# The samples' delta-state update of a gated-DeltaNet step: TensorE outer products replaced by rows spread over the partitions through DRAM, with the products on ScalarE and the sums on VectorE

## What is computed

```
S'    = exp(g) * S
u     = beta * (v - S'^T k)
o     = S'^T q + (q.k) u
S_new = S' + k u^T            # delta_sample, an output of the step
```

## Time and profile before

| what | value |
|---|---|
| median of three runs | 2118.62 us |
| lowest and highest | 2118.04 and 2120.09 us |
| span of the profiled execution | 2117.8 us |
| PE busy in the span | 2014.8 us, 95% |
| DVE, ACT, POOL busy | 1323.2, 941.4, 76.7 us |
| end of `su_done` to the end of the last addition of the samples' states | 201.35 to 331.5 us |
| first matmul of the feed-forward network | 388.2 us |

### The profile page before, as it was taken

The page is one execution under the profiler, slowest core; times in us unless marked ns, Lnnn a source line. Parts: engine busy times, 40 slices in busy tenths (PEclk is TensorE's granted clock), DMA queues, the critical chain, the costliest instruction groups (busy, mean ns, idle before and its releaser), DMA issues.

```text
span 2117.8 us, 27204 instructions
## 1 busy us (share of the span) xinstructions
PE 2014.8 (95%) x10121; PEld 1571.7 (74%) x10121; DVE 1323.2 (62%) x1367; ACT 941.4 (44%) x824; POOL 76.7 (4%) x94
## 2 busy tenths in 40 slices
PE   6998989899999998999799999999999999999997
PEld 4888965899996532325688888888888888888885
DVE  5854863555433211011488797887978889797884
ACT  3541000444320110000277676766767677676772
POOL 1231111000000000000000000000000000000000
PEclk8997987999999999899699999999999999999998
DMA  6231005355548678563199898998989989898990
GB/s 265 99 101 66 1 1 206 142 179 180 182 157 260 211 246 301 188 230 119 60 358 361 321 342 327 351 363 311 342 324 348 357 317 350 320 344 333 339 353 23
DMA packets 96731, 512.34 MB, mean 242 GB/s; under 512 B 10769, under 2 KB 10898, under 8 KB 44418
## 3 DMA queue, kind: packets, MB, share of 16 engines
q1 hardware_dynamic: 81936, 478.50, 60.9%
q10 hardware_dynamic: 13970, 25.46, 3.7%
q0 software_dynamic: 736, 7.21, 1.0%
HBM read 503.91 MB, written 7.21 MB: 241 GB/s over the span
## 4 chain that ended last, share of the span: by engine, by line
issue 67%; PE 27%; DVE 4%; ACT 1%; DMA 0%; SPq 0%; POOLq 0%; POOL 0%; ACTq 0%; DVEq 0%
PE bank L485 5%; PE bank L486 5%; PE bank L487 5%; PE bank L784 3%; PE bank L718 1%; PE bank L696 1%; PE bank L597 1%; PE bank L641 1%; PE bank L621 1%; PE bank L634 1%; DVE w_lo L1381 1%; PE bank L479 1%; ACT w_hi L1040 1%; DVE scr L1437 0%; PE bank L506 0%
## 5 line engine op out<-in xcount | busy, mean ns | idle before, releaser
L1750 DVE TENSOR_TENSOR w_lo<-raw_w,w_hi 128x2048 fp32r<-128x2048 f32 x336 | 768.8, 2290 | 140.8 <-ACT w_hi L1206 137.6
L1206 ACT ACTIVATE w_hi<-raw_w 128x2048 fp32r<-128x2048 f32 x336 | 644.9, 1920 | 429.0 <-PE bank L948 280.1
L946 PE MATMUL bank<-w_hi,xe_hi 128*128 128x512 f32 x896 | 365.6, 408 | 1.5 <-DVE xe_lo L1808 1.5
L948 PE MATMUL bank<-w_hi,xe_lo 128*128 128x512 f32 x896 | 350.8, 392 | 0.0
L947 PE MATMUL bank<-w_lo,xe_hi 128*128 128x512 f32 x896 | 350.2, 391 | 0.0
L486 PE MATMUL bank<-fh_lo,w_hi 128*128 128x264 f32 x704 | 201.8, 287 | 0.0
L946 PEld LDWEIGHTS bank<-w_hi,xe_hi 128*128 128x128 f32 x896 | 169.0, 189 | 36.0 <-issue 1.8
L948 PEld LDWEIGHTS bank<-w_hi,xe_lo 128*128 128x128 f32 x896 | 168.8, 188 | 36.1
L947 PEld LDWEIGHTS bank<-w_lo,xe_hi 128*128 128x128 f32 x896 | 169.2, 189 | 33.7
L946 PE MATMUL bank<-w_hi,aT_hi 128*128 128x512 f32 x448 | 177.1, 395 | 0.0
L947 PE MATMUL bank<-w_lo,aT_hi 128*128 128x512 f32 x448 | 174.6, 390 | 0.0
(11 more groups left out here) (329 smaller groups left out, 2500.9 us busy)
## 6 DMA issues: line engine op xcount, KB each, us to landing
raw_w<-in_moe SPq DMA_DIRECT2D x336, 1024.0 KB, 4.8
raw_w<-in_ffn_w SPq DMA_DIRECT2D x42, 1024.0 KB, 4.8
ring<-in_k_pages SPq DMA_DIRECT2D x96, 256.0 KB, 3.1
raw_w<-in_gdn_in SPq DMA_DIRECT2D x16, 1024.0 KB, 6.9
ring<-in_v_pages SPq DMA_DIRECT2D x64, 256.0 KB, 4.7
ring<-in_v_pages ACTq DMA_DIRECT2D x64, 256.0 KB, 4.1
ring<-in_att_in SPq DMA_DIRECT2D x4, 2048.0 KB, 7.9
ring<-in_k_pages ACTq DMA_DIRECT2D x32, 256.0 KB, 3.7
```

What stands on the lines that cost most here:

```text
L946: mm(out, hi, move_hi, start=first, stop=False)
L948: return mm(out, lo, move_hi, start=False, stop=last)
L1206: A(w_hi[:, p % SPLIT, :], raw_w[:, p % RAW, :], ACT.Copy).then_inc(split_hi, 1)
L1750: V.tensor_tensor(w_lo[:, p % SPLIT, :], raw_w[:, p % RAW, :], w_hi[:, p % SPLIT, :].bitcast(F32), ALU.subtract).then_inc(split_lo, 1)
```

## The change

The products k u^T leave TensorE. TensorE turns u alone into rows, after level 0 of the inverse (into bank 4, which level 1 may use only once VectorE has copied it out). SP writes the 64 rows of 128 values to a buffer in DRAM (32 KB), waits for that, and reads them back in four transfers of 16 rows each, each spread over all 128 partitions (8 KB per partition, 1 MB per transfer), into two buffers in turn; the third and fourth wait for the additions that read the first and second. ScalarE multiplies the 64 states by their decays (in GpSimd's place) and then the 64 spread rows by their keys, one number per partition, in place. VectorE adds four states at a time, four such additions behind each of the levels 2, 3, 5 and 6. The scaling of `ktok` moves from the head of level 3 to the head of level 1. GpSimd keeps only the two stores.

```diff
+ADD_LEVELS = (2, 3, 5, 6)
...
+        u_dram = nc.dram_tensor("u_dram", [NS * H, DK], F32, kind="Internal").ap()
...
-        wide = decT[0:64]
-        kv_rows = carve(core, 14336, 2, P)[0:64]
-
+        u_rows = decT[0:64, 0, 0:DK]
+
+        u_bc = [carve(hT[:, :, :].rearrange("p k t -> p (k t)"), 0, 16, DK),
+                carve(scr, (QKV + 2 * H) * T, 16, DK)]
...
# SP, behind the loads of gdn_out
+            sp.wait_ge(st_sb, 1)
+            sp.dma_start(u_dram, u_rows).then_inc(u_spread, 16)
+            sp.wait_ge(u_spread, 16)
+            for q in range(4):
+                if q >= 2:
+                    sp.wait_ge(snew, 4 * (q - 1))
+                sp.dma_start(u_bc[q % 2], u_dram[16 * q:16 * q + 16, :].unsqueeze(0).to_broadcast([P, 16, DK]))\
+                    .then_inc(u_spread, 16)
...
# PE, in the levels
+                    if l == 1 and g == 0:
+                        pe.wait_ge(st_sb, 1)
...
+                if l == 0:
+                    pe.wait_ge(sou, 1)
+                    nc.tensor.transpose(bank[4][0:64, 0:P], u_s, ident).then_inc(st_ps, 1)
...
# PE, behind the recurrence
-            pe.wait_ge(sou, 1)
             pe.wait_ge(w_sb, 2)
-            nc.tensor.transpose(bank[0][0:64, 0:P], u_s, ident)
-            nc.tensor.transpose(bank[0][0:64, P:2 * P],
-                                sk, ident).then_inc(st_ps, 1)
-            for i in range(16):
-                pe.wait_ge(st_sb, 2 + i)
-                if i < 2:
-                    pe.wait_ge(u_sb, 4)
-                else:
-                    pe.wait_ge(snew, i - 1)
-                mm(bank[2 + i % 2], kv_rows[:, 1, :], wide[:, i % 2, :], start=True, stop=True).then_inc(sout_ps, 1)
...
# ACT, in front of the copies of the recurrence's outputs
+            act.wait_ge(sread_ps, 1)
+            act.wait_ge(su_done, 1)
+            for i in range(NS * H):
+                ins = A(states[:, i, :], states[:, i, :], ACT.Copy, scale=row_b[:, 1, i:i + 1])
+                if i % 4 == 3:
+                    ins.then_inc(scaled, 1)
+            act.wait_ge(sou, 1)
+            for i in range(NS * H):
+                if i % 32 == 0:
+                    act.wait_ge(u_spread, 16 * (3 + i // 16))
+                u = u_bc[i // 16 % 2][:, i % 16, :]
+                ins = A(u, u, ACT.Copy, scale=sk[:, i:i + 1])
+                if i % 4 == 3:
+                    ins.then_inc(scaled, 1)
...
# POOL
-            pool.wait_ge(sread_ps, 1)
-            pool.wait_ge(su_done, 1)
-            for i in range(8):
-                s = states[:, 8 * i:8 * i + 8, :]
-                G.tensor_tensor(s, s, row_b[:, 1, 8 * i:8 * i + 8].unsqueeze(2).to_broadcast([P, 8, DK]),
-                                ALU.mult).then_inc(sdecayed, 1)
-            pool.wait_ge(st_sb, 1)
-            for i in range(16):
-
-                if i >= 2:
-                    pool.wait_ge(sout_ps, i - 1)
-                G.tensor_tensor(wide[:, i % 2, :].rearrange("p (a v) -> p a v", a=4),
...
# DVE, in the levels
-                if l == 3:
+                if l == 1:
...
+                if l == 0:
+                    dve.wait_ge(st_ps, 1)
+                    V.tensor_copy(u_rows, bank[4][0:64, 0:P]).then_inc(st_sb, 1)
+                if l in ADD_LEVELS:
+                    for n in range(4 * ADD_LEVELS.index(l), 4 * ADD_LEVELS.index(l) + 4):
+                        dve.wait_ge(scaled, 16 + n + 1)
+                        s = states[:, 4 * n:4 * n + 4, :].rearrange("p i n -> p (i n)")
+                        u = u_bc[n // 4 % 2][:, 4 * (n % 4):4 * (n % 4) + 4, :].rearrange("p i n -> p (i n)")
+                        V.tensor_tensor(s, s, u, ALU.add).then_inc(snew, 1)
...
# DVE, behind the recurrence
-            dve.wait_ge(st_ps, 1)
-            V.tensor_copy(kv_rows.rearrange("p r n -> p (r n)"), bank[0][0:64, 0:2 * P]).then_inc(st_sb, 1)
...
-            for i in range(16):
-                dve.wait_ge(sout_ps, i + 1)
-                dve.wait_ge(sdecayed, i // 2 + 1)
-                s = states[:, 4 * i:4 * i + 4, :].rearrange("p i n -> p (i n)")
-                V.tensor_tensor(s, s, bank[2 + i % 2][:, :], ALU.add).then_inc(snew, 1)
```

More of the change, by code:

```diff
@@ L336, in program @@
         core_done = sem("core_done")
-        sdiag, srow_ps, sread_ps, sdecayed, su_done, st_ps, st_sb, sou, sout_ps, snew = (
-            sem("sdiag"), sem("srow_ps"), sem("sread_ps"), sem("sdecayed"), sem("su_done"), sem("st_ps"), sem("st_sb"),
-            sem("sou"), sem("sout_ps"), sem("snew"))
+        sdiag, srow_ps, sread_ps, scaled, su_done, st_ps, st_sb, sou, u_spread, snew = (
+            sem("sdiag"), sem("srow_ps"), sem("sread_ps"), sem("scaled"), sem("su_done"), sem("st_ps"), sem("st_sb"),
+            sem("sou"), sem("u_spread"), sem("snew"))
         osq_done, osum, oroot, o_normed = sem("osq_done"), sem("osum"), sem("oroot"), sem("o_normed")
@@ L1307, in _ @@
             pool.dma_start(convs_out[:, :, CONV_W - 2, :], conv_new[:, :, :]).then_inc(stored, 16)
-            pool.wait_ge(sread_ps, 1)
-            pool.wait_ge(su_done, 1)
-            for i in range(8):
-                s = states[:, 8 * i:8 * i + 8, :]
-                G.tensor_tensor(s, s, row_b[:, 1, 8 * i:8 * i + 8].unsqueeze(2).to_broadcast([P, 8, DK]),
-                                ALU.mult).then_inc(sdecayed, 1)
-            pool.wait_ge(st_sb, 1)
-            for i in range(16):
-                if i >= 2:
-                    pool.wait_ge(sout_ps, i - 1)
-                G.tensor_tensor(wide[:, i % 2, :].rearrange("p (a v) -> p a v", a=4),
-                                kv_rows[:, 0, :].unsqueeze(1).to_broadcast([64, 4, DK]),
-                                ident[0:64, 4 * i:4 * i + 4].unsqueeze(2).to_broadcast([64, 4, DK]),
-                                ALU.mult).then_inc(st_sb, 1)
             pool.wait_ge(snew, 16)
```

## The result

The changed kernel takes 2083.21 us (median of four runs, 2081.00 to 2084.04) against 2119.13 us before (now the median of four runs, 2118.04 to 2120.09): ratio 0.9822, 95% interval 0.9808 to 0.9836, 35.9 us less. The forecast was 2079.0 us, with a range of 2074 to 2088. The profiled execution is the fastest of the four, 2081.0 us with a span of 2079.2 (2117.8 before).

What follows compares the result with a forecast made beforehand. It took VectorE, slowed by GpSimd, to bound the front and the samples' outer products on TensorE the tail. -8.3 - 1.2 + 2.5 - 32.6 = -39.6 us from 2117.8 gives 2078.2, plus 0.8 is 2079.0 us; range 2074.3 to 2088.

Steps and rivals of the forecast that it cites:

- Front: Level 0 of the inverse: without GpSimd's decay VectorE is free sooner, level 1 starts at 208.8 instead of 217.1, 8.3 us gained.
- Keys: Key scaling moved from level 3 to level 1: 1.2 us gained in level 3, nothing lost in level 1.
- the engine is then still on 1.2 GHz: Level 1: TensorE's four Y take 5.98 us instead of 3.74, so it finds the first mask ready.
- low end of the range: Whole kernel: additions free (-2.5) and level 1's Y at 2.4 GHz (-2.2), 2074.3 us.
- Additions: VectorE's 16 additions behind four levels: 0.47 us lost at each of three blocks, 1.1 behind level 6, 2.5 in all.
- Rival 1: Inverse: VectorE becomes the bound, additions all exposed, 11.0 us instead of 2.5, 2087.5 us; chance 0.07.
- Inputs and the way through DRAM: ScalarE's decays and scaled rows, and the spread transfers of u, are ready before the additions need them: no wait.
- rival 3: Spread reads from DRAM are slow, VectorE waits behind levels 2 and 5; slower than before beyond 23.6 us per transfer; chance 0.07.
- Tail: First square to the scale: 36.7 us before, 4.1 after without the outer products, 32.6 us gained.
- Behind the tail: Scale, inversion, spreading and projection: unchanged, with the same 4.3 us gap of TensorE between them.
- Rival 2: Row sums in the tail run at 1.2 GHz and take twice 3.6 us, 2082.6 us; chance 0.08.
- The step from span to median: Whole kernel: the median lies 0.8 us above the profiled span, turning 2078.2 into 2079.0 us.

Runs made afterwards that it cites:

- the pieces: Changed kernel with additions placed singly behind the groups of levels 2 to 5 and key scalings in fours behind level 1's: 2075.84 us.
- the third yardstick: The changed kernel unaltered, run beside the third group of experiments (keys or additions alone split up, further filling): 2081.37 us.
- the second yardstick: The changed kernel unaltered, run beside the second group of experiments (single pieces, filled gap, both together): 2083.39 us.
- the kernel with the front alone: Kernel before with only the 64 state decays moved from GpSimd to ScalarE, outer products left on TensorE: 2110.04 us, ratio 0.9953.
- the last experiment: Changed kernel with single pieces and filled gap, plus one 128-column matmul behind each of the root's eight spreads: 2077.62 us, ratio 0.9799.

## Why the prediction was right, and where it was off

*Front, forecast -8.3.* Right in mechanism, measured -9.25, and -9.1 alone. Counted from `su_done`, the second Z subtraction ended 0.25 us earlier than reckoned; the rest is the clock, which was back at 1.00 before level 1: the last Z products took 0.63 us and not 1.1, and the turn of u 0.1 and not 0.3.

*Keys, forecast -1.2 in level 3 and nothing lost in level 1.* The step "the engine is then still on 1.2 GHz" failed. The Y took 3.74 us, not 5.98, so the 2.2 us that the better clock gave were eaten by a wait of 1.9 for the scaling. Level 1 came out even (12.91 against 12.96) and the forecast's sum held by two errors that cancel, which is luck; the pieces show what was missed. The low end of the range had counted the Y at 2.4 GHz as 2.2 us gained, which the wait shows to be wrong too. In some executions the wait also costs 1.6 us of clock, which the forecast did not have at all. It does not explain on its own why the profiled execution lies 2.2 us under the median of its runs: the third yardstick's profile has no such fall either and is the slowest of its five (2083.38 us), and the second yardstick's has the fall and shares the lowest time of its five (2082.11).

*Additions, forecast +2.5.* Mis-sized by little: 0.48 at levels 3 and 4 as reckoned (0.47), 1.07 behind level 6 as reckoned (1.1), and 0.92 in level 6 instead of 0.47; in all 2.95. In level 6 TensorE waits 0.21 us for a mask, as in levels 3 and 4, and 0.43 us more for a subtraction. (The prediction reads the masks' start in level 3 as 4.05 us after TensorE's first Y; its rows give 244.74 - 240.80 = 3.94, and with that 0.56 per block and not 0.47.) Rival 1 (VectorE as the bound, all 11 us exposed) fell: VectorE could take the whole of the work free of charge, in pieces.

*Inputs and the way through DRAM, forecast free.* Right. The decays and the 32 scalings that follow step at 0.294 us (18.82 / 64), with 0.386 us shown for one; the row of 0.401 was right as a duration and too high as a pace. The Trainium skill, "VectorE: DVE Perf Modes", section "The TRN2 errata — SBUF-src ops pay a fixed extra latency per instruction", gives 350 cycles for 128 elements; the prediction's estimate from it, 0.29 us, is the step that this trace shows. Going against its advice on small tiles cost nothing here, since ScalarE had no other work. The spread reads land in 4.6 and 6.4 us per megabyte, within the forecast's bounds and near the 4.8 us of the feed-forward weights' loads of the same size, so rival 3 fell.

*Tail, forecast -32.6.* Measured -32.36 in the profile.

*Behind the tail, forecast 0, measured +1.46.* The step "the stages behind are unchanged" failed. The eight spreads took 7.41 us and not 6.89, the first 48 records of the projection 13.89 and not 12.95, at the same code and the same 4.33 us gap. In the 2 us in which the spreads start, the granted clock is 0.82 before (340 to 342 us) and 0.53 after (299 to 301). Rival 2 looked for the low clock in the row sums and was wrong there (3.72 us, clock 1.00); the low clock came one stage later. But the loss is not shown to belong to the change: the kernel with the front alone, products and all, has it too (53.47 us), and the changed kernel's three profiles lie between 52.52 and 53.46. What of the 1.46 us the change causes is open.

*The step from span to median, forecast +0.8.* This term was mis-sized. It compares the span of one execution with the median of others; within one execution the time lies 1.7 to 1.9 us above the span in every run on record (2081.0 against 2079.2 for the changed kernel). With 1.8 the forecast would have been 2080.0 us.

In sum the touched stretches give 38.5 us in the profiled pair against 39.6 forecast, and the medians 35.9. The last two numbers differ because the changed kernel's profiled execution lies 2.2 us under its median and the span before, with 1.8 added, 0.5 above its own. What makes executions of the changed kernel differ by such amounts was not found; level 1's clock is one part of it.

## What to carry to other kernels

Work that nobody later needs can still hold the end if it stands in front of needed work in an engine's order; look for the first instruction behind it and ask what that one really waits for. An engine with a fifth of its time free in a tight exchange with TensorE takes extra work at no cost in single pieces between the steps, and at 5 us (here, for 16 additions and 16 scalings) in blocks of 2.4 to 3.2 us. Before a small loss in one pair of profiles is explained, look at the same stretch in the other profiles: here the same kernel differed by 0.9 us in it. Price a wait of TensorE of 2 to 3 us with a possible fall of the clock behind it, and test a filler matmul before trusting it: outside a dependent chain it gained 1.6 to 3.0 us, inside one it cost 6 us, more than half of them its own time in the chain.

## What the runs showed of the hardware

- ScalarE multiplies a 128x128 fp32 tile from and to SBUF by a number per partition every 0.294 us, while each is shown with 0.386 us, and VectorE's instructions beside it keep their 0.6 us step. GpSimd's multiplications of 128x1024 made VectorE's instructions of 64 columns last 1.95 us instead of 0.23.
- A transfer of 1 MB whose source is the same 8 KB of DRAM for all 128 partitions lands in 4.6 to 6.4 us (medians of two buffers), where loads of 1 MB with a source of its own for each partition land in 4.8 (feed-forward weights, median of 42).
- The granted clock behind one and the same wait of 1.92 us fell to 0.50 in two profiles and stayed at 1.00 in four. Behind a wait of 3.35 us in the same exchange it fell in the one profile there is.
- It also fell with TensorE busy without a gap, in a stretch where every other pair of matmuls had only 8 rows on the partitions (0.50 from 300 us on in the last experiment).
